# Expert weight tiles of four chunks of one matrix in place of two chunks of two

## The reference, cut to what matters

```python
for g in range(N_GROUPS):                       # 4 groups of 8 experts
    hid = silu(einsum("bld,edf->blef", h, w_gate[g])) * einsum("bld,edf->blef", h, w_up[g])
    out = out + einsum("blef,ble,efd->bld", hid, comb[:, :, g], w_down[g])
```

## Time and profile before

| what | value |
|---|---|
| median of 3 runs | 1681.47 us (1677.83 to 1685.1) |
| profiled execution | 1680.31 us, its span 1678.5 us |
| mean granted TensorE clock | 0.919 of full speed |
| PE busy | 1430.4 us, 85% of the span |
| VectorE, ScalarE, GpSimd busy | 879.7, 724.3, 607.0 us |
| read from HBM | 234.79 MB, 141 GB/s over the span |
| instructions | 20936, of them 6952 matmuls |

### The profile page before, as it was taken

How to read it: one execution, slowest core, us unless ns; L and a number is a source line. 1 busy time by engine, 2 the same in 40 slices (tenths; PEclk the granted TensorE clock), 3 DMA queues, 4 the chain that set the end, 5 groups by cost and what they waited for, 6 DMA issues and landing times.

```text
span 1678.5 us, 20936 instructions
## 1 busy us (share of the span) xinstructions
PE 1430.4 (85%) x6952; PEld 1173.6 (70%) x6952; DVE 879.7 (52%) x1440; ACT 724.3 (43%) x1212; POOL 607.0 (36%) x326
## 2 busy tenths in 40 slices
PE   6989978878999999986799835537999999799997
PEld 5878866656777777765677634425899997578885
DVE  1563263345878777854229964555666655311012
ACT  4454464443757566646333312125223232344343
POOL 5867676400000000015665415223100003657884
PEclk9999996898999999999899967767999999889998
DMA  7645550343988888953753323222000003535562
GB/s 215 180 132 161 148 151 1 88 137 107 351 278 303 279 297 282 304 178 108 202 158 113 111 68 108 91 73 73 29 1 0 0 0 103 151 105 181 176 191 82
DMA packets 126194, 239.92 MB, mean 143 GB/s; under 512 B 15236, under 2 KB 31286, under 8 KB 125996
## 3 DMA queue, kind: packets, MB, share of 16 engines
q1 hardware_dynamic: 116672, 228.17, 43.0%
q10 hardware_dynamic: 9453, 10.84, 2.1%
HBM read 234.79 MB, written 1.05 MB: 141 GB/s over the span
## 4 chain that ended last, share of the span: by engine, by line
PE 62%; DVE 20%; DMA 10%; ACT 4%; issue 2%; ACTq 0%; SPq 0%; DVEq 0%
PE bank L284 11%; PE bank L286 11%; PE bank L285 11%; DMA work<-proj 6%; DVE work L2007 5%; PE bank L2225 3%; DVE wlo L278 3%; PE bank L2243 3%; PE bank L1342 2%; PE bank L2239 2%; PE bank L2209 2%; PE bank L2741 2%; PE bank L2743 2%; PE bank L2742 2%; DVE work L739 2%
## 5 line engine op out<-in xcount | busy, mean ns | idle before, releaser
L278 POOL TENSOR_TENSOR wlo<-raw,whi 128x1024 fp32r<-128x1024 f32 (+1 forms) x234 | 564.5, 2430 | 834.5 <-ACT whi L273 834.0
L284 PE MATMUL bank<-whi,t0h 128*128 128x512 f32 (+1 forms) x1072 | 443.5, 414 | 85.7 <-POOL wlo L278 65.0
L273 ACT ACTIVATE whi<-raw 128x1024 fp32r<-128x1024 f32 (+1 forms) x366 | 376.9, 1053 | 294.7 <-PE bank L286 230.1
L285 PE MATMUL bank<-wlo,t0h 128*128 128x512 f32 (+1 forms) x1072 | 430.5, 402 | 0.0
L286 PE MATMUL bank<-whi,t0l 128*128 128x512 f32 (+1 forms) x1072 | 430.5, 402 | 0.0
L284 PEld LDWEIGHTS bank<-whi,t0h 128*128 128x128 f32 x1072 | 208.3, 194 | 146.4 <-issue 84.8
L286 PEld LDWEIGHTS bank<-whi,t0l 128*128 128x128 f32 x1072 | 207.1, 193 | 49.1
L285 PEld LDWEIGHTS bank<-wlo,t0h 128*128 128x128 f32 x1072 | 207.9, 194 | 45.2 <-issue 1.4
L278 DVE TENSOR_TENSOR wlo<-raw,whi 128x1024 fp32r<-128x1024 f32 x132 | 157.1, 1221 | 25.2 <-ACT whi L273 24.1
L2007 DVE SCALAR_TENSOR_TENSOR work<-work,proj 128x256 f32<-128x256 f32 x210 | 113.0, 596 | 1.9
L2566 DVE TENSOR_TENSOR work<-bank,const 128x256 f32<-128x256 f32 x112 | 46.7, 423 | 63.8 <-PE bank L2225 61.7
(11 more groups left out here) (415 smaller groups left out, 2050.4 us busy)
## 6 DMA issues: line engine op xcount, KB each, us to landing
raw<-in_w_ff SPq DMA_DIRECT2D x64, 512.0 KB, 3.6
raw<-in_w_exp_down SPq DMA_DIRECT2D x124, 256.0 KB, 4.6
raw<-in_w_in SPq DMA_DIRECT2D x60, 496.0 KB, 3.7
raw<-in_w_in SPq DMA_DIRECT2D x56, 512.0 KB, 3.6
raw<-in_w_exp_gate SPq DMA_DIRECT2D x66, 256.0 KB, 5.1
raw<-in_w_exp_up SPq DMA_DIRECT2D x66, 256.0 KB, 5.9
proj<-in_w_exp_gate SPq DMA_DIRECT2D x62, 256.0 KB, 4.4
proj<-in_w_exp_up SPq DMA_DIRECT2D x62, 256.0 KB, 5.5
```

The lines of the kernel that those rows point to most:

```text
L273: nc.scalar.activation(whi[:, s, 0:width], raw_of(n)[:, 0:width], ACT.Copy).then_inc(hi_ready, 1)
L278: ins = (nc.vector if split_by_vector(n) else nc.gpsimd).tensor_tensor(wlo[:, s, 0:width], raw_of(n)[:, 0:width], whi[:, s, 0:width].bitca ...
L284: nc.tensor.matmul(dst, hi, wh, start=first, stop=False)
L285: nc.tensor.matmul(dst, hi, wl, start=False, stop=False)
```

## The change: what it does

A gate/up tile now holds four chunks of one matrix: tiles 0 and 1 of an expert are chunks 0 to 3 and 4 to 7 of `w_exp_gate`, tiles 2 and 3 those of `w_exp_up`. Each is loaded by one transfer, 4 KB contiguous per partition. A down tile is also one transfer in place of two. `RAW_DONE` counts 16 per tile in the expert stage as elsewhere. In `gate_up` a matmul streams 256 columns of one matrix into its half of the bank; a tile takes 4 chunks x 3 = 12 matmuls, and every one has a weight load of its own, as before. Number, size and order of the tiles stay.

```diff
--- before.py
+++ after.py
@@ -164,7 +164,7 @@
 RAW_DONE, LOW_DONE = [], []
 _shown = [0] * MOE_RING
 for _n in range(Q_END):
-    _shown[slot(_n)] += 32 if Q_MOE <= _n < Q_PLE else 16
+    _shown[slot(_n)] += 16
     RAW_DONE.append(_shown[slot(_n)])
     LOW_DONE.append(sum(split_by_vector(m) == split_by_vector(_n) for m in range(_n + 1)))
 
@@ -1151,18 +1151,15 @@
         ov = {s: sem("over_" + s) for s in ("loaded", "up", "silu", "hid", "turned", "copied", "down", "summed",
                                             "zeroed", "scattered", "added")}
 
-        def gu_loads(sp, n, e, q, u=0, per=0):
-            pairs = []
-            for j, name in enumerate(("w_exp_gate", "w_exp_up")):
-                v = A[name][0].rearrange("g e (p k) n -> p (g e) k n", k=KC)[:, ds(e, 1), 2 * q:2 * q + 2, :]
-                dst = raw_of(n)[:, 512 * j:512 * j + 512].rearrange("p (a k n) -> p a k n", a=1, k=2)
-                pairs.append((dst, v))
-            load(sp, n, pairs, u, per)
+        def gu_load(sp, n, e, q, u=0, per=0):
+
+            name = ("w_exp_gate", "w_exp_up")[q // 2]
+            v = A[name][0].rearrange("g e (p k) n -> p (g e) k n", k=KC)[:, ds(e, 1), 4 * (q % 2):4 * (q % 2) + 4, :]
+            load(sp, n, [(raw_of(n).rearrange("p (a k n) -> p a k n", a=1, k=4), v)], u, per)
 
         def down_load(sp, n, e, c, u=0, per=0):
             v = A["w_exp_down"][0].rearrange("g e (p k) n -> p (g e) k n", k=2)[:, ds(e, 1), c:c + 1, :]
-            load(sp, n, [(raw_of(n)[:, f:f + 512].rearrange("p (a k n) -> p a k n", a=1, k=1), v[:, :, :, f:f + 512])
-                         for f in (0, 512)], u, per)
+            load(sp, n, [(raw_of(n).rearrange("p (a k n) -> p a k n", a=1, k=1), v)], u, per)
 
         U = 12
 
@@ -1174,13 +1171,13 @@
             def block(E, m, i=0, per=0):
                 if not (isinstance(E, int) and E == N_EXP - 1):
                     for q in range(4):
-                        gu_loads(sp, m + q, E + 1, q, i, per)
+                        gu_load(sp, m + q, E + 1, q, i, per)
                     m += 4
                 for c in range(2):
                     down_load(sp, m + c, E, c, i, per)
 
             for q in range(4):
-                gu_loads(sp, Q_MOE + q, 0, q)
+                gu_load(sp, Q_MOE + q, 0, q)
             sp.wait_ge(quarter_done, Q_OUT + 1)
             for J in range(NG):
                 n = first_of(J)
@@ -1372,12 +1369,12 @@
                     pe.wait_ge(hid_ready, E + 1)
                 wait_low(pe, n, u, per)
                 s = n % RING
-                wh, wl = (w[:, s, :].rearrange("p (a k n) -> p a k n", a=2, k=2) for w in (whi, wlo))
-                dst = bank[e_par][:, :].rearrange("p (a n) -> p a n", a=2)
+                dst = bank[e_par][:, DE * (q // 2):DE * (q // 2) + DE]
                 r = slice(par * P, (par + 1) * P)
-                for kk in range(2):
-                    k = 2 * q + kk
-                    mm = times(dst, t0h[:, k, r], t0l[:, k, r], wh[:, :, kk, :], wl[:, :, kk, :], k == 0, k == KC - 1)
+                for kk in range(4):
+                    k = 4 * (q % 2) + kk
+                    f = slice(DE * kk, DE * kk + DE)
+                    mm = times(dst, t0h[:, k, r], t0l[:, k, r], whi[:, s, f], wlo[:, s, f], k == 0, k == KC - 1)
                 mm.then_inc(quarter_done, 1)
 
             def turn_hidden(E, e_par):
```

## The result

The changed kernel takes 1687.18 us (median of 20 runs, 1679.23 to 1693.61) against 1682.71 us (20 runs) for the kernel before: ratio 1.003, 95% interval 1.0017 to 1.0043. It lost 5.0 us (2.9 to 7.2) where 4.5 us of gain were forecast. It was profiled twice: one execution of 1693.61 us with a span of 1691.8 us, and one of 1682.69 us with a span of 1680.9 us. In the first, 5.8 us of the excess were already there at the load of `w_out`, ahead of every changed instruction. So I read both traces, and compare distances inside a trace, not its ends.

What follows compares the result with a forecast made beforehand. The prediction took the expert stage to be bound by the PE (8.6 us an expert) with transfers close by (9.3 us). Products +0.5 and transfers -5 summed to -4.5 us, median 1681.47 to 1677.0 us, range 1667 to 1693.

Steps and rivals of the forecast that it cites:

- Which stage, and what bounds it: Expert stage: the PE at 8.6 us an expert and the transfers at 9.3 us are two bounds close together.
- Gate and up products, +0.5 us: Expert stage: 768 matmuls of 0.2333 us become 1536 of 0.117 us, 179.2 us to 179.7, +0.5 us.
- The rival in which the load shows: Gate/up matmuls: weight loads not hidden, interval 0.140 us, about +26 us, 1707 us; chance 0.15.
- the fixed 20 ns: Gate/up matmuls: each pays a fixed 20 ns, interval 0.127 us, +7 us, 1688 us; chance 0.12.
- Transfers, -5 us: Expert tile loads: one transfer in 4 KB runs returns half of the PE's 10.3 us of waits for low parts, -5 us.
- A loss is excluded for this part: Expert tile loads: no loss possible, since tiles always needed their second transfer and 4 KB packets cost no more per byte.
- nothing should move outside of it: Whole kernel: the expert stage gets 3 to 7 us shorter and no other part changes.
- an interval of 0.115 to 0.119 us: Sign in the new trace: spacing between gate and up matmuls; 0.125 us or more would make the prediction wrong.
- a packet of about 180 ns: Sign in the expert stage's DMA queue: time that a 4 KB packet should take.
- ScalarE's wait was to fall below 18 us: Sign in the expert stage: ScalarE waits less than 18 us for expert tiles in place of 26.4.
- the stage to be 3 to 7 us shorter: Sign in the trace: the expert stage shortens by 3 to 7 us.
- the transfers bring nothing: Expert tile loads: queue stalls, not run length, set when tiles land, so only +0.5 us remains, 1682 us; chance 0.12.

Runs made afterwards that it cites:

- x3: Kernel before, but only the first half of every expert tile is loaded, by one transfer of 2 KB runs; 512-column products kept: 1671.71 us, 0.9952 of before.
- y2: Kernel before with one of three gate/up products (low parts left out), so the PE has slack; loads of before: 1669.0 us, 0.9927 of before.
- x4: Changed kernel's 256-column products with only the first half of every expert tile loaded, by one transfer of 2 KB runs: 1677.06 us, 0.9977 of before.
- z1: Kernel before with a ring of twelve raw slots in place of six; tiles, loads and products stay: 1675.08 us, 0.9947 of before.
- z2: Changed kernel with a ring of twelve raw slots in place of six; tiles, loads and products stay: 1677.44 us, 0.9962 of before.
- y3: One of three gate/up products, as in y2, but with the change's loads in 4 KB runs: 1663.19 us, 0.9888 of before.
- x2: Changed kernel's one-matrix tiles and 256-column products, but each tile loaded by two transfers in 2 KB runs: 1684.54 us, 1.0017 of before; repeated, 1686.06 us, 1.0022.
- y1: Kernel before with only the down tiles loaded by one transfer in 4 KB runs; gate/up tiles stay two transfers: 1682.25 us, 0.9996 of before.

## Why the prediction was wrong

The measured 1687 us lies inside the stated range of 1667 to 1693, but only because the range is wide: the change loses time where a gain was forecast.

**Which stage, and what bounds it: right.** The prediction had the PE at 8.6 us an expert and the transfers at 9.3. x3 and y2 take one each away and show the other, at 8.79 and 9.01 us.

**Gate and up products, +0.5 us: right in kind, mis-sized.** The load does hide, as said, and a 256-column interval is just above the 0.117 taken: 0.1183 us. But the step multiplies it by 1536, and so 1.3 ns are 2 us, and the intervals give +2.7 us. The stage itself shows less, +1.8 and +1.7 us in the two pairs without late tiles (x3 and x4, z1 and z2). By the prediction's own working the excess over the columns is 11.6 ns at 256 and 19.8 at 512, so part of it does go with each matmul. The Trainium skill ("TensorE: Matmul & The Clock Gate", Back-to-back issue gap) gives N/2.4 + 2.5 ns for one isolated matmul, which is 109 ns at 256 columns. In these back-to-back streams the trace has 118 ns there, and 233 at 512 columns where that formula has 216. The rival in which the load shows (0.140) and the fixed 20 ns (0.127) are both out.

**Transfers, -5 us: the step that failed.** "What that returns lies between nothing and the 10.3 us that the PE waits for low parts ... I take half". It is nothing: the kernels with the loads alone are 3.2 us slower than before (about 1.8 to either side), with stages of 329.5 and 328.6 us for 329.0 before; down tiles alone were -0.7 us, within 2 of nothing. The 10.3 us were the wrong measure of what transfers can return, too: 7.3 of them stay when no tile is late. That all late tiles together cost 8 us, not far from 10.3, is luck. The packets did get lighter, as the feed-forward rows said, by 5% in place of 6%. What was wrong is the link from a packet to a wait. ScalarE's wait for a tile is not the PE's: in the second trace it fell by 7.5 us, the PE's by 0.9. A tile is asked for when a slot comes free, and that is when VectorE has split the tile six back; I take it that when it lands then depends on the queue's state after the last gather or scatter, which an average of 9.3 against 8.7 us an expert does not tell. The rows had a sign of it: share 102.4% in one stretch and 0.70 in another. SyncE's 158.9 us of waiting for slots are no such sign, since with twelve slots they are 164.7. The ring of z1 gives what I had asked of the longer runs, and some 4 us more (0.53%, 8.9 us). By the Trainium skill ("DMA: Bandwidth & Descriptors", Specifications) line rate begins at 512 B, so that 4 KB runs would gain nothing over 2 KB. The trace does not quite agree: a packet of 4 KB takes 5% less per byte, and y3's stage is 5.0 us shorter than y2's; in the kernel as it is the gain is nothing.

**"A loss is excluded for this part" and "nothing should move outside of it": wrong.** Another queue was running on the same engines. Four microseconds of the DMA queues, from 8.6 us behind the first expert load on; before, 352 to 356 us, and after, 357.8 to 361.8:

```profile
q1 hardware_dynamic: 281, 0.52, 35.9%
q10 hardware_dynamic: 468, 0.48, 33.0%
```

```profile
q1 hardware_dynamic: 137, 0.50, 42.7%
q10 hardware_dynamic: 368, 0.22, 17.2%
```

and x2, 355.3 to 359.3 us, also from 8.6 us behind its first expert load:

```profile
q1 hardware_dynamic: 185, 0.35, 42.7%
q10 hardware_dynamic: 315, 0.17, 15.3%
```

SyncE's queue moves 0.5 MB as before, ScalarE's 0.22 MB in place of 0.48; in x2 both move less. So the router's loads come 1.6 to 2.3 us later. What makes it so is not settled. It is not the run length, since x2 has 2 KB runs and a copy at 16.8; and not the down tiles (y1). It goes with full gate/up tiles from one matrix each: with half of their bytes (x3) the copy is at 15.0. Nor are the engines short of time in these windows. The two shares add up to 69%, 60% and 58%, while a megabyte of SyncE's queue takes more engine time: of the 16 x 4 = 64 us in a window, 0.359 x 64 / 0.52 MB = 44 us before, 55 after, 78 in x2. So the packets themselves are slower. Whether that is the place in HBM from which both queues read or the order in which the engines serve them, no run here tells apart.

**What would show it.** Two of the signs came: an interval of 0.115 to 0.119 us (0.1183) and a packet of about 180 ns (185). Two did not: ScalarE's wait was to fall below 18 us (25.5 and 18.9), and the stage to be 3 to 7 us shorter (5.6 longer and 0.5 shorter).

**The sum.** Products +1.8 by the stage or +2.7 by the intervals, the late copy +1.3, transfers 0: +3.1 to +4.0 of the 5.0 measured (2.9 to 7.2). What the loads alone cost beyond the late copy, 1.9 us give or take 1.8, has no cause that a trace shows. The rival "the transfers bring nothing" had the failed step right, with a chance of 0.12, and no case of the prediction had the late copy.

## What to carry to other kernels

A transfer made lighter pays only where its queue binds the tile that someone waits for. Half the bytes tell what all late tiles cost, and which waits stay without any; where the queue is full in one place and half empty in another, try more slots first. How long the issuer waits for slots does not tell. A price per instruction that is multiplied by a thousand must be known to a nanosecond, or the range must carry it. Before calling a stage's loads free of side effects, list the other queues that run beside the first of them, and let no early wait include loads that are needed late.

## What the runs showed of the hardware

- Back-to-back float32r matmuls of 256 columns with a 128-wide weight load each follow at 0.1183 us at the clock of 2.4 GHz, those of 512 at 0.2331: the doubled loads hide, and each half of a split matmul takes 1.8 ns more than half of the old interval.
- A 4 KB packet takes 0.185 us and a 2 KB packet 0.097 in the same stage, yet 2 KB runs reach 368 GB/s in an expert of z1. With the PE out of the way the loads of the change are worth 0.1 us in an ordinary expert of 9 and 5.0 us over the stage (y2, y3).
- What one queue fetches delays another, even with the engines not full: with the same 0.5 MB in 4 us on SyncE's queue, ScalarE's moved 0.22 MB in place of 0.48, at a summed share of 0.60 for 0.69.
